# A decoder layer's opening: tokens turned by products with a diagonal of inverse roots, and the first projection begun after three token tiles

## The reference, cut to what matters

```
def rms_norm(x, g):
    xf = x.astype(jnp.float32)
    y = xf * lax.rsqrt(jnp.mean(xf * xf, axis=-1, keepdims=True) + RMS_EPS)
    return (y * g.astype(jnp.float32)).astype(x.dtype)

def decoder_layer(x, ...):
    h = rms_norm(x, g_mix)
    proj = h @ w_in
    q, k, v, u, gate_a, gate_s = jnp.split(proj, ...)
    # then stick-breaking attention, an S5 state-space branch, a gated merge with
    # w_out, a squared-ReLU MLP and gated per-layer embeddings, each added to x
```

## Time and profile before

| | |
|---|---|
| median of 3 runs | 980.76 us (979.64 to 985.96) |
| the profiled execution | 981.12 us, its span 979.3 us |
| PE busy | 952.0 us, 97% of the span |
| DVE, ACT, POOL busy | 596.7, 440.6 and 63.0 us |
| the chain that ended last | 92% PE, 4% ACT, 2% DVE, 2% issue, 1% DMA |
| first matmul of the second unit | at 28.43 us |

### The profile page before, as it was taken

The page is one execution under the profiler, slowest core; times in us unless marked ns, Lnnn a source line. Parts: engine busy times, 40 slices in busy tenths (PEclk is TensorE's granted clock), DMA queues, the critical chain, the costliest instruction groups (busy, mean ns, idle before and its releaser), DMA issues.

```text
span 979.3 us, 17811 instructions
## 1 busy us (share of the span) xinstructions
PE 952.0 (97%) x7508; PEld 912.6 (93%) x7508; DVE 596.7 (61%) x808; ACT 440.6 (45%) x663; POOL 63.0 (6%) x111
## 2 busy tenths in 40 slices
PE   5999999999999989999999999999999999999998
PEld 4989899989788879999999999999999999999997
DVE  6498789723354542646556766666667666777543
ACT  6334233224455454453436554444444444445532
POOL 5000022310100050010000000000000000000000
PEclk8999999999899999999999999999999999999999
DMA  9422223822552139342222222222222222242202
GB/s 221 120 65 66 75 90 98 194 77 76 149 156 68 46 119 360 120 144 65 84 86 70 83 86 87 87 88 86 87 87 87 86 87 87 87 151 80 75 2 97
DMA packets 131016, 99.85 MB, mean 102 GB/s; under 512 B 15400, under 2 KB 121240, under 8 KB 130904
## 3 DMA queue, kind: packets, MB, share of 16 engines
q1 hardware_dynamic: 124392, 81.02, 28.4%
q0 software_dynamic: 5424, 17.65, 5.7%
q10 hardware_dynamic: 1120, 0.04, 0.1%
HBM read 87.53 MB, written 11.03 MB: 101 GB/s over the span
## 4 chain that ended last, share of the span: by engine, by line
PE 92%; ACT 4%; DVE 2%; issue 2%; DMA 1%; SPq 0%; ACTq 0%; DVEq 0%
PE dense L2028 62%; PE banks L2028 20%; PE scoreA L2028 4%; PE scoreB L2028 3%; PE banks L2159 3%; ACT whi L1144 1%; DMA xtok<-in_x_prompt 1%; ACT xsq L1268 0%; PE dense L2159 0%; DVE mt L1586 0%; ACT ga L1457 0%; DVE mt L1512 0%; ACT yh L1464 0%; DVE sm L1911 0%; ACT act_hi L1279 0%
## 5 line engine op out<-in xcount | busy, mean ns | idle before, releaser
L1536 DVE TENSOR_TENSOR wlo<-wraw,whi 128x1024 fp32r<-128x1024 f32 (+1 forms) x139 | 148.6, 1072 | 73.8 <-ACT whi L1144 61.3
L2028 PE MATMUL dense<-hid,whi 128*128 128x256 f32 (+1 forms) x1024 | 176.1, 294 | 0.1
L2028 PE MATMUL dense<-act_hi,whi 128*128 128x256 f32 (+1 forms) x736 | 162.9, 302 | 1.8 <-DVE R L1613 1.0
L2028 PE MATMUL dense<-act_hi,wlo 128*128 128x256 f32 (+1 forms) x736 | 157.4, 295 | 0.0
L2028 PE MATMUL dense<-act_lo,whi 128*128 128x256 f32 (+1 forms) x736 | 156.6, 294 | 0.0
L2028 PEld LDWEIGHTS dense<-hid,whi 128*128 128x128 f32 x1024 | 152.5, 188 | 0.5 <-issue 0.5
L2028 PEld LDWEIGHTS dense<-act_hi,whi 128*128 128x128 f32 x736 | 122.1, 190 | 8.7 <-issue 5.8
L1144 ACT CAST whi<-wraw 128x1024 fp32r<-128x1024 f32 x100 | 104.8, 1049 | 45.4 <-PE banks L2028 44.3
L2028 PEld LDWEIGHTS dense<-act_hi,wlo 128*128 128x128 f32 x736 | 123.4, 189 | 0.0
L2028 PEld LDWEIGHTS dense<-act_lo,whi 128*128 128x128 f32 x736 | 122.5, 188 | 0.0
L2028 PE MATMUL dense<-hid,wlo 128*128 128x256 f32 (+1 forms) x512 | 108.9, 294 | 0.0
(11 more groups left out here) (344 smaller groups left out, 1562.3 us busy)
## 6 DMA issues: line engine op xcount, KB each, us to landing
wraw<-in_w_in SPq DMA_DIRECT2D x32, 512.0 KB, 4.3
wraw<-in_w_up SPq DMA_DIRECT2D x32, 512.0 KB, 4.0
wraw<-in_w_down SPq DMA_DIRECT2D x32, 512.0 KB, 3.6
gates_spill<-gst POOLq DMA_DIRECT2D x16, 288.0 KB, 2.4
page<-in_cache_k SPq DMA_DIRECT2D x16, 256.0 KB, 3.2
page<-in_cache_v SPq DMA_DIRECT2D x16, 256.0 KB, 5.7
wraw<-in_w_out SPq DMA_DIRECT2D x8, 512.0 KB, 4.0
wraw<-in_w_ple_gate SPq DMA_DIRECT2D x8, 512.0 KB, 4.1
```

Source lines behind the costliest of these rows:

```text
L1536: return nc.vector.tensor_tensor(out=lo, in0=whole, in1=f32(hi), op=ALU.subtract)
L2028: return nc.tensor.matmul(out, lhsT, rhs, start=start, stop=stop, skip_group_check=True)
```

## The change

It does four things.

- VectorE no longer scales a tile. It scales the 128 x 128 identity by the inverse roots of the tile's tokens (`diag`), and TensorE multiplies the raw tile by that (`mm` in place of `transpose`): turning and scaling are one product. The products wait for `xn_ready`, which is now `diag`'s, and for the tile itself.
- The first projection unit is cut in four stages. Three of them (tokens 0 to 255: `act_hi` with `whi`, `act_hi` with `wlo`, `act_lo` with `whi`) stand as events `first` between the tiles' products: after tile 2, after tile 3 and after tile 4. What is left of the unit is tokens 256 to 575.
- In the list `scale 2` stands behind tile 0's banks, `split_hi 0` ahead of tile 1's, `split_lo 0` and `hlo 0` after tile 2's, with `scale 3`, `square 4`, `hlo 1` and `scale 4` behind them.
- Tile 1 of x is issued by ScalarE's queue, as its first instruction, ahead of the table load and of the gain's DMA.

```diff
--- before.py
+++ after.py
@@ -205,27 +205,39 @@
         for half in range(2):
             event("h", t, half, place=(2 * t + half) % 4)
 
-    for t in range(3):
-        event("square", t)
-        event("scale", t)
+    event("square", 0)
+    event("scale", 0)
+    event("square", 1)
+    event("scale", 1)
+    event("square", 2)
     tokens(0)
+    event("scale", 2)
+    event("split_hi", 0)
+    tokens(1)
     event("square", 3)
-    tokens(1)
-    event("split_hi", 0)
+    tokens(2)
+    dense_job(("m", 0, 0))
+    event("first", 0)
+    event("split_lo", 0)
+    event("hlo", 0)
+    event("scale", 3)
     event("square", 4)
-    tokens(2)
-    event("scale", 3)
-    event("split_lo", 0)
+    event("hlo", 1)
     event("scale", 4)
     tokens(3)
+    event("first", 1)
     tokens(4)
-    for t in range(5):
+    event("first", 2)
+    for t in range(2, 5):
         event("hlo", t)
     event("split", 1)
     event("split", 2)
     job("qs0", 0)
     job("qs1", 1)
-    unit()
+    flush()
+    event("unit", 0)
+    consumed(("split", 0))
+    n[0] += 1
     unit()
     event("qksum", 0)
     unit()
@@ -635,6 +647,7 @@
         xtok = placed(58880, "xtok", [P, 5, D])
         xsq = placed(58880 + 20480, "xsq", [P, D])
         hf = placed(58880 + 24576, "hf", [P, 5, 2, 4, P])
+        diag = placed(58880 + 45056, "diag", [P, 5, P])
 
         gnat = placed(50688, "gnat", [P, GP, CH, GC])
         up_ = placed(50688, "uchunk", [P, 2, 8, CH, GC])
@@ -886,7 +899,7 @@
                                cache[0][bass.ds(page, 1)].rearrange("a r h d -> (a r) (h d)")).then_inc(
                                    page_in[n % NPAGE], 16)
 
-            for t in range(5):
+            for t in (0, 2, 3, 4):
                 tokens(t)
             for u in range(NRAW):
                 weights(u)
@@ -1253,6 +1266,7 @@
                 scalar.wait_ge(last_gate, part + 1)
                 nc.scalar.activation(ysg[:, 1, c0:c1], yf[:, 1, c0:c1], ACT.Sigmoid).then_inc(count.up(ysg_ready), 1)
 
+            scalar.dma_start(xtok[:, 1, :], i["x_prompt"][0][P:2 * P, :]).then_inc(x_in[1], 16)
             nc.scalar.preload_act_table_set("sqrt_and_others")
             scalar.dma_start(gains[:, 0, :], i["g_mix"][0].rearrange("(k p) -> p k", p=P),
                              allow_slow_non_contiguous=True).then_inc(gmix_in, 16)
@@ -1639,7 +1653,9 @@
                     nc.vector.reciprocal(stat[0:n, 1, t:t + 1], stat[0:n, 0, t:t + 1]).then_inc(
                         count.up(dve_steps), 1)
                     vector.wait_ge(*count.last)
-                    nc.vector.tensor_scalar(xtok[0:n, t, :], xtok[0:n, t, :], stat[0:n, 1, t:t + 1], None,
+                    if t == 0:
+                        vector.wait_ge(ident_ready, 1)
+                    nc.vector.tensor_scalar(diag[0:n, t, 0:n], ident[0:n, 0:n], stat[0:n, 1, t:t + 1], None,
                                             ALU.mult).then_inc(count.up(xn_ready), 1)
                 elif k == "h":
                     t, half = a
@@ -2047,7 +2063,7 @@
                     return pT
                 return act
 
-            def first_unit():
+            def first_unit(stage):
 
                 slot = jobs["m", 0, 0][0] - DENSE
                 wh, wl = [wview(w, 0, 0) for w in (whi, wlo)]
@@ -2059,16 +2075,22 @@
                                  start=start and k == 0, stop=stop and k == KT - 1)
                     return ins
 
-                tensor.wait_ge(h_hi, 4)
-                sweep(0, wh, act[0], start=True)
-                sweep(0, wl, act[0])
-                tensor.wait_ge(h_hi, 10)
-                sweep(1, wh, act[0], start=True)
-                sweep(1, wl, act[0])
-                tensor.wait_ge(h_lo, 4)
-                sweep(0, wh, act[1], stop=True)
-                tensor.wait_ge(h_lo, 10)
-                sweep(1, wh, act[1], stop=True).then_inc(full_of(("m", 0, 0)), 1)
+                if stage == 0:
+                    tensor.wait_ge(w_hi, 1)
+                    tensor.wait_ge(h_hi, 4)
+                    sweep(0, wh, act[0], start=True)
+                elif stage == 1:
+                    tensor.wait_ge(w_lo, 1)
+                    sweep(0, wl, act[0])
+                elif stage == 2:
+                    tensor.wait_ge(h_lo, 4)
+                    sweep(0, wh, act[1], stop=True)
+                else:
+                    tensor.wait_ge(h_hi, 10)
+                    sweep(1, wh, act[0], start=True)
+                    sweep(1, wl, act[0])
+                    tensor.wait_ge(h_lo, 10)
+                    sweep(1, wh, act[1], stop=True).then_inc(full_of(("m", 0, 0)), 1)
 
             begun = {}
 
@@ -2079,7 +2101,7 @@
                     tensor.wait_ge(w_lo, turn["split", u])
                 x = operand(u)
                 if u == 0:
-                    first_unit()
+                    first_unit(3)
                     return
                 if u == FIRST["attn"]:
                     tensor.wait_ge(so_low, 4)
@@ -2174,15 +2196,16 @@
                 if k == "h":
                     t, half = a
                     n = TOK[t][1]
-                    if t == 0 and half == 0:
-                        tensor.wait_ge(ident_ready, 1)
+                    tensor.wait_ge(x_in[t], 16)
                     tensor.wait_ge(xn_ready, t + 1)
                     if used_before(e):
                         tensor.wait_ge(*free(e))
                     for c in range(4):
                         c0 = P * (4 * half + c)
-                        ins = transpose(bank(e)[:, P * c:P * c + n], xtok[0:n, t, c0:c0 + P], n)
+                        ins = mm(bank(e)[:, P * c:P * c + n], xtok[0:n, t, c0:c0 + P], diag[0:n, t, 0:n], True, True)
                     ins.then_inc(full_of(e), 1)
+                elif k == "first":
+                    first_unit(a[0])
                 elif k == "prod":
                     product(*a)
                 elif k == "s5ct":
```

## The result

The changed kernel takes 984.16 us (983.0 to 984.78, five runs) against 980.35 for the one before in the same comparison: ratio 1.0033, 95% interval 1.0017 to 1.0049. No change beyond one per cent, as forecast; but 3.8 us slower (1.7 to 4.8 by the interval), where the forecast was 0.9 above its own base of 980.76. The profiled execution took 983.0 us.

What follows compares the result with a forecast made beforehand. TensorE's unbroken stream bounds the kernel, so its start counts: tile 3 turned from 18.0 at half speed, VectorE ending the opening at 28.9 to 29.7, taken as 29.3 against 28.43, +0.9 us. Forecast 981.7 us; 8-in-10 range 979.0 to 985.0.

Steps and rivals of the forecast that it cites:

- The frame: Opening: the second unit's start, 28.43 us before, carries through one for one; VectorE ends the opening, forecast at 29.3.
- The mis-sized term: VectorE's path to tile 3: tile 2's banks by 15.1, `wlo`, `act_lo`, reciprocal and diagonal to 18.0, then turning starts.
- my two ends of tile 2: End of tile 2's products on TensorE: 14.2 if the clock rose near 10.6, 15.8 if near 14.
- my two cases: When the clock first rises in the opening: near 10.6 or near 14 us.
- They should be there: The gain's 4 KB, behind tile 1 on ScalarE's queue, come later but in time for `hf` at 9.3 us.
- the falls of the clock after 246 and 356 us: Two later falls, 6.8 and 3.4 us long, costing 3.4 and 1.7 us; a shifted opening may move them either way.
- The clock stays up: Rival, 20%: no fall of the clock in the opening; second unit at 26.5, -1.9 us, 978.9 us.
- The clock stays down: Rival, 15%: lower clock through the 24 matmuls of 320 tokens behind tile 4; +4.5 us, 985.3 us.
- No dearer than a transpose: Rival, 5%: a product costs no more than a transpose when turning tiles; -1.6 us, 979.2 us.
- the doubled price: Turning a tile by products: eight take 1.7 us at full or 3.4 at half speed, against 0.9 or 1.75 by transposes.
- the sweeps as costing nothing: Three sweeps move 24 of the first unit's 48 matmuls into TensorE's gaps, costing nothing as long as there is a gap.

Runs made afterwards that it cites:

- experiment 12: Changed kernel with 22 short idle products on TensorE while it waits for x; 983.31 us, ratio 1.0011.
- experiment 1: Changed kernel with tile 1 of x issued by SyncE (SP's queue) again; 982.58 us, ratio 1.0027.
- experiment 2: Changed kernel with the gain's DMA put ahead of tile 1's on ScalarE's queue; 984.32 us, ratio 1.0042.
- experiment 4: Kernel before with the diagonal and products alone, its order, undivided first unit and queues kept; 981.42 us, ratio 1.0011.
- experiment 3: Changed kernel with whole tiles scaled by VectorE and turned by transposes again, new order and queues kept; 985.27 us, ratio 1.0046.
- 6: Changed kernel with tile 1 issued by SyncE and the first unit's three sweeps all behind tile 4's products; 984.43 us, ratio 1.006.
- 9: Kernel before with diagonal and products alone, plus 22 short idle products on TensorE while it waits for x; 980.12 us, ratio 0.999.
- 7: Kernel before with 80 satisfied waits at the head of TensorE's list, which became 40 more instructions; 981.16 us, ratio 1.0008.
- 11: Kernel before with 42 short idle products on TensorE, 168 more instructions; 980.7 us, ratio 0.9994.
- experiment 5: Changed kernel with tile 1 issued by SyncE, tile 3's square ahead of the weights' rounding and its diagonal ahead of `wlo`; 983.19 us, ratio 1.0036.

## Why the prediction was right in sign and short in size

**The frame held.** The second unit's start carries through one for one (in experiment 12 its 2.5 us stay to the end), but for falls of the clock that last longer or shorter later on. VectorE's `wlo` ends the opening, at 30.88 before 31.08. Products are two instructions (48 for 24 of them), and a tile takes about 1.7 us at the upper clock and 3.3 at the lower (16 x 0.21). Tile 3 is turned behind a hole, mostly at the lower clock, which is back 4 us later. From tile 3's first product to the second unit I had 29.3 - 18.0 = 11.3 us; it took 31.08 - 19.72 = 11.36. There is some luck in that: tile 3 took 2.90 us and not 3.4, but tile 4's eight products took 1.93 at the upper clock, where I had 1.7 even at the lower.

**The mis-sized term: "VectorE has tile 2's banks by 15.1 ... reciprocal and diagonal to 18.0. Tile 3 is turned from 18.0".** It was 19.72, and this is the whole of the opening's error (1.72 of 1.78 us). All but 0.02 of it is there when `wlo` begins, at 16.80 and not at 15.1, and it has two parts. The 15.1 is the middle between my two ends of tile 2, 14.2 and 15.8, and the products ended late in that range: the sweep behind them starts at 15.91, 0.9 later. For this TensorE started at 7.92 and not 7.35, since the first square stood at 5.78 and not 5.3, and the clock rose at about 13.4, near the later of my two cases. The other 0.8 is a term that I left out: between the last product and a free VectorE stand the last bank's way and its `hf` (16.20 to 16.89), which I had counted for tile 4 but not here. What follows took what I had said, 2.92 us for 2.9.

**The gain.** "They should be there" by 9.3: it landed near 11.7, 10.4 us after its issue, and VectorE waited 1.87 us. That is a wrong statement that cost nothing in the traces: TensorE ran on from 7.92 to 16.16 without a pause, and in experiment 1, with the gain there in time, tile 3 moved by no more than TensorE's start did.

**The term that I did not have: the hole at 425 us**, 1.17 us. I put the falls of the clock after 246 and 356 us into the range, but nothing that the count of instructions could do 400 us on. With it, 0.87 foreseen, 1.78 unforeseen in the opening and 1.17 make the 3.8 us.

**The rivals.** "The clock stays up" missed for the changed kernel; the reason given against it, the hole ahead of tile 3, does not settle it, since in experiment 2 the clock stays up through the same hole. It is also what happens in experiment 4, where the same products stand in the old order. "The clock stays down" did not come: the clock was back at 23.7, before the matmuls of 320 tokens. In experiments 3 and 6 it stayed down for over 13 us, so it was near. "No dearer than a transpose" was wrong.

**What I had put wrongly as a lesson.** I read the doubled price as the change's loss and the sweeps as costing nothing. By the traces: products in the old order -1.4 us; the new order on top +3.1, of which two places hold 1.66; the second queue +0.94. Together -1.38 + 3.09 + 0.94 = +2.65; that this closes is no test, since each term is the step from one trace to the next. The medians divide the +3.8 otherwise: +0.95 (with a hole of 1.1), +1.2 and +1.7, each uncertain by over 1 us, so how large each term is in a usual run stays open. The sweeps between the tiles are no loss: without them the second unit is 3.4 us later and the median 2.0 higher. In the prediction I cited the Trainium skill, "Perfetto Trace Analysis", section "Transposes", for the transpose against the product. In this opening its advice is not borne out, for the product does the scaling too and keeps TensorE at work: in the old order the second unit begins at 27.05 and 27.63 with products (4 and 9), at 28.43, 27.67 and 28.98 with transposes (before, 7 and 11). The medians do not tell the two apart there. As to the Trainium skill, "TensorE: Matmul & The Clock Gate", Part 4, by which transposes do not count as busy for the clock, the rows of before spoke against it, and experiment 3 does too, where the clock rose at 11.8 after nothing but transposes. But in experiments 7 and 11 the same transposes as in the kernel before were turned at half speed throughout, and the clock rose only at 22.6 and 25.5, after the first sweeps had begun. So transposes can bring the clock up, and do not always; the runs don't show what decides.

**What stays open**: why the median of experiment 5 stayed 1.4 us above its profiled execution, how often each kernel has the fall at 212 to 220 us, and what makes the clock rise or fall at another time over the same work. Experiment 9 is the best version, with the diagonal in the old order and the hole moved away, but its interval takes in 1.

## What to carry to other kernels

In an opening where TensorE works with gaps, ask of an edit first whether it keeps TensorE at work; a dearer instruction in a gap can be cheaper than the clock that a gap costs. When an order is rewritten, look for the late landing and list what now stands behind it on its engine: here one tile's square and diagonal. Read an opening in more than one trace, since the clock alone moved it by 0.7 us over the same work, and hold what the traces say against the medians. And after an edit that adds instructions, pair the two traces to the end, since a difference far away may come with their number.

## What the runs showed of the hardware that was not expected

- A transfer of 4 KB in pieces of 4 bytes takes 10.4 us to land behind 512 KB on its queue, against 5.1 alone; and 512 KB behind it take 8.3 us instead of the 5.1 that they take first in the queue.
- With two queues side by side the first tile was squared at 5.78 instead of 4.71 us: the second tile's early landing seems to be paid by the first. With the second tile behind the 4 KB (experiment 2) it was squared at 4.78.
- A wait that is already met costs TensorE some 0.1 us as an instruction of its own (88 of them from 1.9 to 11.5 us), and of these every two had become one.
- A float32 product with 64 columns took 0.22 us per instruction before the clock rose, as much as one with 128 (0.21), and one with 4 columns and 32 weight columns 2.51 / 44 = 0.06.
- The number of TensorE's instructions makes or removes a hole of up to 1.2 us, 400 us later, always at the same place in its list and 1.4 to 1.55 us after a 16 KB transfer of the instruction queue ends.
- Over the same work of TensorE the clock first rose at 14.0, 22.6 or 25.5 us (before, 7, 11), and at 12.8 or 9.7 (1, 6).
- The same hole of 2.63 us was followed by a fall of the clock in the changed kernel and by none in experiment 2.
